# Fourth mixer of a two-block transformer kernel: its attention and retention steps placed between half units of its in-projection

## The reference, cut to what matters

```python
def even_mixer(h, w_in, w_out, q_norm_g, k_norm_g, rel_bias, pos):
    proj = h @ w_in
    rq, rk, rv, rg, aq, ak, av = jnp.split(proj, EVEN_SPLITS, axis=-1)
    rq = rotary(rq.reshape(B_, S, RET_HEADS, RET_DIM), pos)
    rk = rotary(rk.reshape(B_, S, RET_HEADS, RET_DIM), pos) * (RET_DIM ** -0.5)
    ret = retention(rq, rk, rv.reshape(B_, S, RET_HEADS, RET_VDIM))
    ret = head_rms(ret).reshape(B_, S, RET_VW).astype(h.dtype) * jax.nn.silu(rg)
    aq = rms_norm_2(aq.reshape(B_, S, ATT_HEADS, ATT_DIM), q_norm_g)
    ak = rms_norm_2(ak.reshape(B_, S, ATT_HEADS, ATT_DIM), k_norm_g)
    att = chunk_attention(aq, ak, av.reshape(B_, S, ATT_HEADS, ATT_DIM), rel_bias)
    return jnp.concatenate([ret, att], axis=-1) @ w_out
```

## Time and profile before

| | us |
|---|---|
| three runs | 2266.87, 2268.89, 2272.28 |
| their median | 2268.89 |
| the profiled execution | 2268.3 |
| its span (first to last instruction) | 2266.4 |
| PE busy in it | 2185.8 |
| DVE busy | 1589.6 |
| ACT busy | 1122.4 |

### The profile page before, as it was taken

The page is one execution under the profiler, slowest core; times in us unless marked ns, Lnnn a source line. Parts: engine busy times, 40 slices in busy tenths (PEclk is TensorE's granted clock), DMA queues, the critical chain, the costliest instruction groups (busy, mean ns, idle before and its releaser), DMA issues.

```text
span 2266.4 us, 35819 instructions
## 1 busy us (share of the span) xinstructions
PE 2185.8 (96%) x15182; PEld 1995.5 (88%) x15182; DVE 1589.6 (70%) x1750; ACT 1122.4 (50%) x1404; POOL 6.7 (0%) x16
## 2 busy tenths in 40 slices
PE   9999999999999999989999979999999999999998
PEld 7888888768999999989999958899898888889997
DVE  4896686346777777648776445888887545888887
ACT  4222231345344543445334436677776555667775
POOL 0000000000000000000000000000000000000000
PEclk9999999999999999999999989999999999999999
DMA  8576767514887788536885512688887332788885
GB/s 316 198 242 242 283 229 257 207 56 149 309 292 276 261 290 301 203 130 250 308 306 199 184 73 94 234 302 314 297 307 280 124 114 111 279 296 299 315 310 211
DMA packets 126740, 535.51 MB, mean 236 GB/s; under 512 B 11744, under 2 KB 47912, under 8 KB 82416
## 3 DMA queue, kind: packets, MB, share of 16 engines
q1 hardware_dynamic: 124896, 524.33, 64.4%
q0 software_dynamic: 944, 5.72, 0.7%
q10 hardware_dynamic: 736, 3.10, 0.4%
HBM read 532.04 MB, written 1.06 MB: 235 GB/s over the span
## 4 chain that ended last, share of the span: by engine, by line
PE 84%; DVE 8%; ACT 4%; issue 2%; DMA 1%; SPq 0%; DVEq 0%; ACTq 0%
PE PS L924 16%; PE PS L1399 13%; PE PS L850 11%; PE PS L996 8%; PE PS L1433 7%; PE PS L946 7%; PE PS L885 5%; PE PS L1051 4%; DVE moe_low L2584 3%; PE PS L1357 2%; PE PS L1335 1%; PE PS L819 1%; PE PS L751 1%; PE PS L984 1%; DMA ring<-mod_w 1%
## 5 line engine op out<-in xcount | busy, mean ns | idle before, releaser
L924 PE MATMUL PS<-h_parts,FFN_HIGH 128*128 128x256 f32 x2112 | 383.1, 284 | 2.9 <-DVE h_parts L2138 2.9
L2584 DVE TENSOR_TENSOR moe_low<-moe_ring,W_HIGH 128x2048 fp32r<-128x2048 f32 x128 | 292.9, 2290 | 76.7 <-ACT W_HIGH L1905 76.7
L924 PEld LDWEIGHTS PS<-h_parts,FFN_HIGH 128*128 128x128 f32 x2112 | 328.9, 192 | 3.7 <-issue 3.4
L924 PE MATMUL PS<-h_parts,ring_low 128*128 128x256 f32 x1056 | 298.7, 283 | 0.0
L1399 PE MATMUL PS<-moe_low,HXH 128*96 128x256 f32 x1008 | 282.7, 280 | 0.0
L1905 ACT ACTIVATE W_HIGH<-moe_ring 128x2048 fp32r<-128x2048 f32 x128 | 244.6, 1913 | 23.1 <-PE PS L1433 21.8
L2165 DVE TENSOR_TENSOR ring_low<-ring,FFN_HIGH 128x2048 fp32r<-128x2048 f32 x99 | 226.8, 2291 | 39.9 <-ACT FFN_HIGH L1651 39.9
L2196 DVE SCALAR_TENSOR_TENSOR roots<-CB,cond_rows,roots 128x1024 f32<-128x1024 f32 x186 | 238.3, 1281 | 8.9
L1651 ACT ACTIVATE FFN_HIGH<-ring 128x2048 fp32r<-128x2048 f32 x99 | 189.0, 1909 | 102.4 <-DMA ring<-down_w 92.0
L924 PEld LDWEIGHTS PS<-h_parts,ring_low 128*128 128x128 f32 x1056 | 202.4, 192 | 0.0
L1399 PEld LDWEIGHTS PS<-moe_low,HXH 128*96 128x96 f32 x1008 | 164.2, 163 | 0.3
(11 more groups left out here) (358 smaller groups left out, 4976.5 us busy)
## 6 DMA issues: line engine op xcount, KB each, us to landing
moe_ring<-moe_w SPq DMA_DIRECT2D x192, 1024.0 KB, 5.0
CB<-mod_rows SPq DMA_DIRECT2D x192, 512.0 KB, 5.9
ring<-up_w SPq DMA_DIRECT2D x88, 1024.0 KB, 5.0
ring<-lin_w SPq DMA_DIRECT2D x55, 1024.0 KB, 4.9
ring<-down_w SPq DMA_DIRECT2D x43, 1024.0 KB, 5.9
CB<-mod_dual SPq DMA_DIRECT2D x96, 128.0 KB, 2.6
ring<-mod_w SPq DMA_DIRECT2D x8, 1024.0 KB, 8.9
CB<-mod_rows SPq DMA_DIRECT2D x32, 128.0 KB, 3.0
```

What stands on the lines that cost most here:

```text
L924: return mm(PS[:, i % 2, h * S:(h + 1) * S], a[:, k, h * P:(h + 1) * P], b[:, k, :], start=start, stop=(k == KT - 1 and j == 2), skip_grou ...
L2584: tt(by_tile(moe_low[:, moe_slot(l, p), :]), by_tile(moe_ring[:, moe_slot(l, p), :]), w_high_tiles(p), ALU.subtract).then_inc(w_low, 1)
```

## The change

The 14 units come in the order aq0, ak0, aq1, ak1, av0, av1, rq0, rk0, rq1, rk1, rv0, rv1, rg0, rg1. PE, ACT and DVE each walk 28 steps; a step of PE is half a unit and then what the tables below name for that step. ACT and DVE do their part of it one or two steps later in their own queues, ahead of the copy and the rest of the weight unit that is due. There are three buffers for the rounded copies (in memory of `CB`, of a table that is no longer used, and of `SG`), two from unit 8 on. The function table EXP_LN is loaded at the start of the mixer and SILU ahead of the last two units, which are the gates. The turned probabilities of a round stand in one PSUM bank for both heads, in two pairs of buffers, and the scores of a round take banks 0 and 1 alone (before: four banks in turn). All arithmetic is the same.

```diff
+E_UNITS = (("aq", 0), ("ak", 0), ("aq", 1), ("ak", 1), ("av", 0), ("av", 1), ("rq", 0), ("rk", 0), ("rq", 1), ("rk", 1),
+           ("rv", 0), ("rv", 1), ("rg", 0), ("rg", 1))
+E_SPLIT_AT = {2 * (i - 2) if i < 10 else 2 * (i - 1): i for i in E_BUFFER}
+E_SCORES = (7, 9, 10, 12, 13, 15, 16, 18)
+E_TURNS = tuple(n + 2 for n in E_SCORES)
+E_OUT = tuple(n + 4 for n in E_SCORES)
+E_MEANS, E_ROTATIONS = (2, 4, 6, 8), (14, 16, 18, 20)
+E_RET_SCORES, E_RET_OUT, E_RET_MEANS = (18, 20, 22, 22), (22, 24), (23, 25)
...
             def mixer_e():
-                by_features("e_in", 10, 0, 0, 6)
-                by_tokens("e_in", 4, 10, 10)
-                pe.wait_ge(lin_ready, LIN_TILE0["e_in"] + 14)
-                rotation(E_QK, 2048, "rot_half")
...
+                for n in range(E_STEPS):
+                    half_unit("e_in", E_UNITS, 6, n // 2, n % 2)
+                    if n in E_OUT:
+                        outputs(E_OUT.index(n))
+                    if n in E_TURNS:
+                        turns(E_TURNS.index(n))
+                    if n in E_MEANS:
+                        mean_squares(E_MEANS.index(n))
+                    if n in E_ROTATIONS:
+                        turn_pairs(E_ROTATIONS.index(n))
+                    if n in E_RET_OUT:
+                        retention_out(E_RET_OUT.index(n))
+                    if n in E_RET_MEANS:
+                        retention_means(E_RET_MEANS.index(n))
+                    for h in range(4):
+                        if n == E_RET_SCORES[h]:
+                            retention_scores(h)
+                    if n in E_SCORES:
+                        scores(E_SCORES.index(n))
                 pe.wait_ge(cat_ready, 4)
-                attention("e")
                 pe.wait_ge(at_kept, 8)
                 out_proj("e_out", 7)
```

More of the change, by code:

```diff
@@ L721, in _ @@
             ffn(3)
-            stream("e_in", 14, lin_w, LIN0["e_in"])
+            for i, (kind, c) in enumerate(E_UNITS):
+                load(UNIT0["e_in"] + i, 0, 0, UNIT0["e_in"] + i + 1, UW, source(lin_w, LIN0["e_in"] + E_FIRST[kind] + c))
             stream("e_out", 4, lin_w, LIN0["e_out"])
@@ new lines, in split_e, with squares_of @@
+                def split_e(i):
+                    u = UNIT0["e_in"] + i
+                    act.wait_ge(full[u % SLOTS], landed(u))
+                    act.wait_ge(unit_done, UNIT0["e_in"] + (E_BEFORE[i] + 1 if i in E_BEFORE else 0))
+                    af(in_high("e_in", i), by_tile(ring[:, u % SLOTS, 0:UW]), ACT.Copy).then_inc(w_high, 1)
+                def squares_of(c):
+                    kind, h = E_UNITS[c]
+                    at = E_COLS[kind] + h * BANK
+                    act.wait_ge(lin_ready, LIN_TILE0["e_in"] + c + 1)
+                    if c >= 2:
+                        act.wait_ge(hms_psum, HEAD0["e"] + c - 1)
+                    af(E_SQ[c % 2], E_QK[:, at:at + BANK], ACT.Square).then_inc(hsq_ready, 1)
@@ new lines, in roots_of @@
+                def roots_of(which, c):
+                    act.wait_ge(hms_psum, HEAD0[which] + c + 1)
+                    if which == "r":
+                        act.wait_ge(hn_ready, HEAD0["e"] + 4)
+                    elif c >= 2:
+                        act.wait_ge(hn_ready, HEAD0["e"] + c - 1)
+                    w = E_WIDE[c % 2]
+                    line(af(w, PS[:, 4, :], ACT.Ln, bias=eps[:, 0:1]))
+                    line.wait()
+                    af(w, w, ACT.Exp, scale=-0.5).then_inc(hr_ready, 1)
@@ new lines, in probabilities, with turned @@
+                def probabilities(r):
+                    W = at_width("e", r % 2)
+                    for s in (2 * r, 2 * r + 1):
+                        act.wait_ge(at_max, 8 + r + 1)
+                        p = E_PROBS[:, s % 6, 0:W]
+                        af(p, p, ACT.Exp, bias=at_col("neg", s), accum_out=at_col("sum", s)).then_inc(at_exp, 1)
+                def turned(r):
+                    W = at_width("e", r % 2)
+                    act.wait_ge(at_tpsum, 16 + 2 * r + 2)
+                    for half in range(2):
+                        if r >= 2:
+                            act.wait_ge(at_out, 16 + 2 * r - 2)
+                        af(E_PT[:, 2 * (r % 2) + half, 0:W], PS[:, 2, half * S:half * S + W], ACT.Copy).then_inc(at_tready, 1)
@@ L1830, in mixer_e @@
+                load_table(SILU)
+                evacuate_e(12)
+                evacuate_e(13)
                 out_parts(7, at_kept, 8, cat_ready, 4)
@@ new lines, in scaled, with normed @@
+                def scaled(r):
+                    W = at_width("e", r % 2)
+                    dve.wait_ge(at_exp, 16 + 2 * r + 2)
+                    line(dve.reciprocal(at_col("inv", 2 * r, 2), at_col("sum", 2 * r, 2)))
+                    line.wait()
+                    for s in (2 * r, 2 * r + 1):
+                        p = E_PROBS[:, s % 6, 0:W]
+                        ts(p, p, at_col("inv", s), None, ALU.mult).then_inc(at_probs, 1)
+                def normed(c):
+                    kind, h = E_UNITS[c]
+                    at = E_COLS[kind] + h * BANK
+                    t = E_QK[:, at:at + BANK]
+                    dve.wait_ge(hr_ready, HEAD0["e"] + c + 1)
+                    stt(out=t, in0=t, scalar=small[:, 24:25] if kind == "aq" else col("ak_gain"), in1=E_WIDE[c % 2],
+                        op0=ALU.mult, op1=ALU.mult).then_inc(hn_ready, 1)
```

262 lines of the change are left out of this document (207 added, 55 removed).

## The result

| | us |
|---|---|
| changed kernel, four runs | 2245.61, 2248.99, 2250.64, 2253.50 |
| their median | 2249.81 |
| kernel before, four runs beside them, median | 2270.59 |
| ratio | 0.9914, interval 0.9901 to 0.9926 |
| profiled execution (span) of the changed kernel | 2253.50 (2251.6) |

A forecast was written before the change was run, and what follows sets the result against it. No engine was full in mixer e's 55.45 us tail, a relay of waits; PE remains the bound. Less 33.1 us of products and waits of 1.4, 0.4 and 1.5, 19.0 us are gained: 2249.9 us, range 2246 to 2258.5.

The forecast's parts named there:

- Place and kind of the gain: Mixer e's 55.45 us tail, a relay of engines awaiting each other, moves between in-projection half units; PE stays the bound.
- Plain products: PE's inserted retention, rotation and head-mean products between half units cost 15.5 us at the full clock.
- Attention: Attention's scores, turning and values between half units cost PE 4.0 us per two rounds, four times: 16.0 us.
- Changing kinds: Nine in-projection half units behind narrow products each take 0.18 us more, 1.6 us together.
- Start: At the first head mean PE waits 1.4 us for ACT's squares, behind table loads and the copy of unit 2.
- Rounds: In attention, round 1's way through ACT and DVE takes 7.2 us against PE's 6.8: a wait of 0.4 us.
- End: Ahead of the out-projection PE waits 1.5 us for the last gate unit's way out, its product and handovers.
- Sum: 55.45 less 33.1 of products and waits of 1.4, 0.4 and 1.5 gives 19.0 us gained, 2249.9 in the median.
- rival 1: Relay misses its windows: three rounds wait 1.5 us each, other steps 2 together, one clock drop: 2257.7 us; chance 0.17.
- rival 5: Slower: PE's queue stops in all 8 attention rounds, 2.6 us plus 1.7 for the clock each: 2284 us; chance 0.03.
- Clock: PE's clock stays 1.00 between half units; waits of 1.4 and 1.5 us don't drop it; each drop costs 1.7 us.

The follow-up runs named there:

- x9_fill: Kernel before, with unread idle PE products ahead of attention and a pair in each attention pass but the first: 2271.56 us, ratio 1.0016 to the kernel before.
- x2_noload: Changed kernel without the two function table loads at the mixer's start: 114.32 us from first in-projection to first out-projection product, 1.49 shorter.
- x5_delay1: Changed kernel with one unread 0.7 us DVE pass ahead of each of eight probability scalings: 117.23 us from first in-projection to first out-projection product.
- second comparison: Changed kernel unaltered, five more runs beside nine of the kernel before (2268.74 us): 2250.88 us, ratio 0.9925.
- x6_delay3: Changed kernel with three unread DVE passes (2.2 us) ahead of each of the eight probability scalings: one run of 2257.89 us.
- x7_ret: Changed kernel with rotations and retention moved behind the last half unit, norms and attention staying between half units: 2263.19 us, ratio 0.9969 to the kernel before.
- x1_busy: Kernel before, with unread idle PE products, seven behind the rotations and four behind the retention means: 2273.80 us, ratio 1.0017 to the kernel before.

## Why the prediction was right, step by step

- **Place and kind of the gain**: right. The relay's time was PE's idle time, and it is gone. PE remained the bound, the clock was 1.00 from 1244 to 1355, and no rival happened. The out-projection begins at 1353.99; the forecast was 1355.6.
- **Plain products** (forecast 15.5): 16.2. Those of retention, norms and rotation have the 0.43 a product that the earlier trace rows gave. The rest is restarts: 1.12 instead of 0.86 behind the wait, 1.92 instead of 1.73 and 1.05 instead of 0.86 behind narrow products.
- **Attention** (forecast 16.0): 14.2, the term that was mis-sized. Two rounds take 0.63 + 0.42 for scores, 1.09 + 0.45 for turning, 0.59 + 0.37 for values, 3.55 in all; I had read 4.0 from starts to starts of the earlier trace rows. Those rows stand in a relay: the turning of the 128-key round (0.65) stands behind a wait of 0.57 and takes 0.45 without one, and the scores are 0.1 cheaper. The lesson is to price a piece that moves to a dense place from rows without a wait ahead of them. The busy times of the earlier trace rows would not have done: they overlap and add up to 4.15.
- **Changing kinds** (forecast nine times 0.18, 1.6): exactly that. Nine half units take 3.06 (two of them 3.05 and 3.07), all behind narrow products; the rest 2.88. About the same 0.19 is in the rotation and the retention values above and in each turning of a 256-key round, 1.09 behind values against 0.89 behind the idle products of `x9_fill`.
- **Start** (forecast a wait of 1.4): 1.24, plus 0.26 for the first product behind it. On ACT the two loads take 1.28 us each with 0.01 between and behind them. The Trainium skill (ScalarE: Activation LUTs, What ACT_TABLE_LOAD costs) adds a drain of about 1380 ns to a load; this trace doesn't agree: ACT's last activation ends at 1242.94, the two loads run from 1242.96 to 1245.53, and the copy starts at 1245.54. The 1.49 us of `x2_noload` say nothing on this, since without the loads PE comes later than ACT.
- **Rounds** (forecast 0.4): 0. The longest way ends 0.11 us inside its window, by `x5_delay1`, where I had it 0.4 outside. PE's window is 6.9 us (its scores end at 1274.15, the turning begins at 1281.05), as I had it (6.8). The way through ACT and DVE is the shorter one, since the turning can begin when the first of the two scalings is done, and I had counted both. The mechanism, copy and rest ahead of the scaling, is as described.
- **End** (forecast 1.5): 1.48.
- **Sum**: the forecast had 36.4 us beyond the plain in-projection, the trace 34.55. That the median still is within 0.1 us of 2249.9 is luck, in a spread of 7.9 us over four runs. The profiled execution was forecast at 2249.3 and took 2253.5: the stage gained 1.9 more, the rest of the program was 5.8 us longer than in the profile the sum was made against, and the in-projection began 0.3 later; and the median of the four lies 3.7 below that execution. Against the runs of the kernel before beside it, the gain is 20.8 us by medians and 17.9 in the second comparison, where 19.0 were forecast.
- **Rivals**: `x6_delay3` gives the price of rival 1 and bounds rival 5. With 2.2 us more in every round, only four of eight wait (the fourth and those from the sixth on don't) and the loss is 9.0 us, not 34. Rival 5 was further off than I had put it.
- **Clock**: I placed waits of 1.4 and 1.5 on the good side, "not far" from a drop. Behind dense products waits of 1.24, 1.48 and 1.60 us left it at 1.00; those of 1.76 and 2.08 were followed by 0.50 for two to three microseconds. The 1.82 of `x7_ret` doesn't tell, as a hole of 4.75 came 1.1 us later. The length of the last wait alone doesn't decide either: in `x1_busy` the clock fell between waits of 1.32 and 0.64 us. The Trainium skill (TensorE: Matmul & The Clock Gate, Part 1) has the array drop when idle and return under sustained work; the rows agree, and `x9_fill` shows that keeping it up with idle work won nothing here.

## What to carry to other kernels

Where one engine does dense work and then waits through a relay of three, put the relay's steps between pieces of the dense work, and price it as: the length of the relay before, less the relay's products at the dense rate, less one wait for each end. Then look at the two ends, since the middle hides itself: here they were a table load and a wait for eight tiles where four were ready, 3 us for a few lines. Idle products to hold a clock were no substitute here: in one stretch they moved the drop into the next, and in both they cost what they gave.

## What the runs showed of the hardware that I had not expected

- A drop of the clock that was filled away came back a few microseconds later: `x1_busy` kept 1.00 up to attention, lost it within attention (0.50 from 1355 to 1365) and again at its end, and was slower than before in the end, 0.7 us in the stage and 2.5 in the out-projection.
- A first product behind a wait costs about 0.25 us more: 1.12 instead of 0.86 (512 columns), 0.71 instead of 0.45 (four turning products).
- Two function-table loads back to back take 2.57 us, with no pause around them.
- The same code behind the mixer took 891.6 to 897.6 us in different profiles with an out-projection at full clock, along with how far the clock fell in short handovers; stage times between two products of PE repeated to 0.01 us in both kernels that were profiled twice.
